# One inference step of a hybrid decoder trunk: split weights outside the experts, interleaved element by element

## What is computed

```python
# layer 0
q, fl, v, gate = split(rmsnorm(x) @ hgrn_w_in, 4)          # 1024 x 4096
o = recurrence(silu(q), 1 - f, v, log f)                   # f from fl
x = x + (headnorm(o) * g_norm * silu(gate)) @ hgrn_w_out   # 1024 x 1024
xn = rmsnorm(x)
x = x + (silu(xn @ ffn_w1) * (xn @ ffn_w3)) @ ffn_w2       # 1024 x 3584, twice, and 3584 x 1024
# layer 1
b, c, h = split(rmsnorm(x) @ conv_w_in, 3)                 # 1024 x 3072
x = x + (b * conv3(c * h)) @ conv_w_out                    # 1024 x 1024
x = x + sum over 8 experts of gate_e * swiglu(rmsnorm(x), w1[e], w3[e], w2[e])
y = rmsnorm(x)
```

## Time and profile before

| | |
|---|---|
| median of three runs (lowest, highest) | 1505.19 us (1504.82, 1506.57) |
| the profiled execution's own time | 1508.43 us |
| its span, first to last instruction | 1506.6 us |
| mean granted TensorE clock | 0.995 |
| busy: TensorE matmuls, weight loads | 1479.1 us, 1297.6 us |
| busy: VectorE, ScalarE, GpSimd | 1236.9 us, 962.0 us, 83.8 us |
| moved by DMA | 483.97 MB, 321 GB/s |

### The profile page before, as it was taken

How to read it: one execution, slowest core, us unless ns; L and a number is a source line. 1 busy time by engine, 2 the same in 40 slices (tenths; PEclk the granted TensorE clock), 3 DMA queues, 4 the chain that set the end, 5 groups by cost and what they waited for, 6 DMA issues and landing times.

```text
span 1506.6 us, 23455 instructions
## 1 busy us (share of the span) xinstructions
PE 1479.1 (98%) x8803; PEld 1297.6 (86%) x8804; DVE 1236.9 (82%) x906; ACT 962.0 (64%) x693; POOL 83.8 (6%) x65
## 2 busy tenths in 40 slices
PE   9998999999999999999999999999999999999997
PEld 8987899999999978888888888888888888888885
DVE  6898866656578779889888888888888888988987
ACT  6644353333353567777777777777777777777774
POOL 1035200000000030000000000000000000000300
PEclk9999999999999999999999999999999999999998
DMA  8745697888654669999999999999999999999990
GB/s 311 225 131 157 221 342 267 305 297 300 228 182 168 228 227 413 403 367 389 376 381 382 373 393 375 377 385 376 382 392 359 387 395 361 388 385 364 407 413 36
DMA packets 212938, 483.97 MB, mean 321 GB/s; under 512 B 8810, under 2 KB 26314, under 8 KB 209820
## 3 DMA queue, kind: packets, MB, share of 16 engines
q1 hardware_dynamic: 209224, 473.67, 85.2%
q10 hardware_dynamic: 2388, 5.32, 1.0%
q0 software_dynamic: 1280, 4.33, 0.7%
HBM read 446.45 MB, written 36.87 MB: 321 GB/s over the span
## 4 chain that ended last, share of the span: by engine, by line
PE 86%; DVE 1%; issue 0%; ACT 0%; DVEq 0%
PE Q L2544 20%; PE Q L2495 14%; PE Q L2497 14%; PE Q L2496 14%; PE Q L2039 7%; PE Q L2040 7%; PE Q L2041 7%; PE Q L2528 2%; DVE wlo L1174 1%; PE Q L2474 0%; PE Q L2505 0%; ACT yrows L1149 0%; PE Q L2400 0%; PE Q L2408 0%; PE Q L2032 0%
## 5 line engine op out<-in xcount | busy, mean ns | idle before, releaser
L1174 DVE TENSOR_TENSOR wlo<-raw,whi 128x2048 fp32r<-128x2048 f32 x413 | 940.3, 2297 | 186.2 <-ACT whi L988 109.3
L988 ACT ACTIVATE whi<-raw 128x2048 fp32r<-128x2048 f32 x336 | 642.2, 1919 | 169.8 <-PE Q L2497 81.1
L2495 PE MATMUL Q<-whi,xgh 128*128 128x512 f32 x896 | 354.2, 395 | 0.0
L2497 PE MATMUL Q<-whi,xgl 128*128 128x512 f32 x896 | 349.6, 390 | 0.0
L2496 PE MATMUL Q<-wlo,xgh 128*128 128x512 f32 x896 | 348.9, 389 | 0.0
L2039 PE MATMUL Q<-xh,whi 128*128 128x264 f32 x1024 | 294.7, 288 | 5.4 <-DVEq L1285 1.8
L2040 PE MATMUL Q<-xl,whi 128*128 128x264 f32 x1024 | 292.0, 285 | 0.0
L2041 PE MATMUL Q<-xh,wlo 128*128 128x264 f32 x1024 | 290.7, 284 | 0.0
L2039 PEld LDWEIGHTS Q<-xh,whi 128*128 128x128 f32 x1024 | 193.8, 189 | 8.1 <-issue 4.1
L2497 PEld LDWEIGHTS Q<-whi,xgl 128*128 128x128 f32 x896 | 168.1, 188 | 35.8
L2496 PEld LDWEIGHTS Q<-wlo,xgh 128*128 128x128 f32 x896 | 168.5, 188 | 33.6
(11 more groups left out here) (286 smaller groups left out, 1138.8 us busy)
## 6 DMA issues: line engine op xcount, KB each, us to landing
raw<-in_moe_w SPq DMA_DIRECT2D x336, 1024.0 KB, 7.1
raw<-in_ffn_w SPq DMA_DIRECT2D x42, 1024.0 KB, 7.3
raw<-in_hgrn_w_in SPq DMA_DIRECT2D x16, 1024.0 KB, 7.3
xg_rows<-zeros SPq DMA_DIRECT2D x6, 2048.0 KB, 10.9
y_rows<-zeros SPq DMA_DIRECT2D x6, 2048.0 KB, 11.7
raw<-in_conv_w_in SPq DMA_DIRECT2D x12, 1024.0 KB, 5.4
raw<-in_hgrn_w_out SPq DMA_DIRECT2D x4, 1024.0 KB, 5.0
raw<-in_conv_w_out SPq DMA_DIRECT2D x4, 1024.0 KB, 5.1
```

The costliest lines, as they stand in the source:

```text
L988: a.activation(bufs(q)[0], raw[:, n % RAW, PW * (q % 2):PW * (q % 2 + 1)], ACT.Copy).then_inc(hi_done, 1)
L1174: v.tensor_tensor(low, raw[:, slot, PW * half:PW * (half + 1)], high.bitcast(F32), ALU.subtract).then_inc(lo_done, 1)
L2495: t_.matmul(out, xgh[:, kt, :], high[:, w], start=(kt == 0), stop=False)
L2497: mm = t_.matmul(out, xgl[:, kt, :], high[:, w], start=False, stop=(kt == DT - 1))
```

## The change

The two tiles `whi` and `wlo` become one tile `wp` with a last axis of 2: for each slot, element and pair, the high part stands at the even and the low part at the odd position. The names `whi` and `wlo` are now views of it, so that every use outside the experts, which is written with these names, has a step of 8 bytes from one float to the next. For the experts a second tile `wm` lies over the same memory, with the two parts of a slot one behind the other, and `bufs` uses it for slots 0 to 2; there each part is contiguous as before. A slot covers the same 16 KB in both readings. The three slots of the experts' own, `whi2` and `wlo2`, stay. No instruction is added, removed or moved.

```diff
--- before.py
+++ after.py
@@ -90,8 +90,10 @@
 
         raw_at = top[0]
         raw = keep("raw", [P, RAW, CW])
-        whi = keep("whi", [P, SPLIT, PW], F32R)
-        wlo = keep("wlo", [P, SPLIT, PW], F32R)
+        w_at = top[0]
+        wp = keep("wp", [P, SPLIT, PW, 2], F32R)
+        wm = at("wm", [P, SPLIT, 2, PW], F32R, w_at)
+        whi, wlo = wp[:, :, :, 0], wp[:, :, :, 1]
         xT_at = top[0]
         xT = keep("xT", [P, DT, T])
         xn_at = top[0]
@@ -230,7 +232,7 @@
         def bufs(q):
 
             b = MOE_SLOT[q % SPLIT_M]
-            return (whi[:, b, :], wlo[:, b, :]) if b < SPLIT else (
+            return (wm[:, b, 0, :], wm[:, b, 1, :]) if b < SPLIT else (
                 whi2[:, b - SPLIT, :], wlo2[:, b - SPLIT, :])
 
         Q = [ctx.enter_context(nc.psum_tensor(f"Q{i}", [P, 4, 512], F32)) for i in range(2)]
```

## The result

The changed kernel takes 1511.87 us in the median of 7 runs (1509.91 to 1514.26), the kernel before 1505.19 in 7 runs beside it (1504.50 to 1507.86). The ratio is 1.004 with a 95% interval of 1.0028 to 1.0052: slower by 6.0 us, between 4.2 and 7.8. On another chip, against 20 runs of the kernel before with median 1506.37, the changed kernel took 1510.92 and the ratio was 1.0025 (1.0015 to 1.0035). So the change costs 0.25 to 0.4%, some 4 to 6 us. The predicted 1505 us and "no change" are wrong; the measured time lies in the range of 1502 to 1530.

A forecast was written before the change was run, and what follows sets the result against it. The prediction took TensorE's queue as the bound, with the moving operand's stream and not the load setting the pace. Its four points summed to 0 + 0 + 0 + 0, so 1505 us, with a range from 1502 to 1530.

The forecast's parts named there:

- no change: Whole kernel: the likeliest case, 1503 to 1507 us, chance 0.74, with 1505 us as the predicted time.
- Point 1, weight loads: 3744 dense matmuls outside the experts load stepped blocks: bounded by 0 and +341 to 397 us, taken as 0.
- the row that it leaned on: Transposes' loads of unstepped 4-byte floats, 139 to 140 ns: read as 0.44 ns a column, 16 bytes in 1.76 ns.
- the argument by rates: Dense weight loads: a stepped load must cross 16 bytes in 1.68 ns, nearly the rate seen on both read sides.
- the doubling of +341 to 397 us: Dense weight loads: a load taking twice as long a column becomes the bound, 1846 to 1902 us, chance 0.10.
- the cover: Dense matmuls: a load of some 106 ns lies 15 ns under the 121.2 ns between two matmuls.
- The signs: Dense loads at 188 to 189 ns would show the forecast right, loads above about 204 ns point 1 wrong.
- the small penalty: Dense loads 13 to 27 ns longer, slightly over their cover: 0 to 100 us, around 1550 us, chance 0.07.
- Point 2, VectorE: VectorE's subtractions outside the experts, stepped reads and writes: 0 to 0.5 us more per 2048 elements, taken as 0.
- Point 3, ScalarE: ScalarE's stepped copies outside the experts: between 0 and a doubling (+1.7 us each), taken as 0.
- Point 4, experts: Expert slots 0 to 2 keep each part contiguous, with steps and lengths as before: 0, stage stays at 953 us.
- The rival on VectorE and ScalarE: Either engine slower on its stepped side, unhidden in the first 200 us: 1508 to 1530 us, chance 0.06.

The follow-up runs named there:

- narrow_step1: Kernel before, with the second and third matmul of each dense group of three streaming only 128 of 264 columns, loads without a step: 1502.69 us, ratio 0.9967.
- load_step2: Kernel before, with only TensorE's weight loads outside the experts stepping by 8 bytes: 1511.49 us against 1507.4, ratio 1.003.
- experts_too: Changed kernel, with the experts' slots 0 to 2 interleaved too, so their moving operand steps by 8 bytes: 1966.39 us, ratio 1.3055 to the kernel before.
- write_step2: Changed kernel, with ScalarE and VectorE still stepping but TensorE loading 128 floats without a step: 1506.6 us, ratio 1.0004 to the kernel before.
- write_again: Second run of the changed kernel in which TensorE loads without a step while ScalarE and VectorE step: 1507.23 us, ratio 1.0005 to the kernel before.
- narrow_step2: Kernel before, with two of three dense matmuls streaming 128 of 264 columns and weight loads stepping by 8 bytes: 1521.61 us, ratio 1.0095.

## Why the prediction was wrong, by its own steps

*What bounds the kernel* held: TensorE's queue, and in the dense stage the pace of one matmul. The statement that the stream alone sets this pace in both stages was too strong. It rested on the first matmul of line 2613 behind a stream of 512 columns, where a load has over 100 ns to spare, and says nothing on 264 columns. There the load is close behind: 121.1 ns against a floor of 108.5 to 111.2 (narrow_step1).

*Point 1, weight loads, is the step that failed.* "Between these I take 0" costed the stepped load at 0, where it is 8 ns a load and 1.4 ns a matmul, 5.2 us in all. Three things went wrong.

First, the row that it leaned on doesn't carry it. The transposes' loads last 139 ns, which was read as 0.44 ns a column. A load of 128 columns would then occupy the loader for 56 ns, but the transposes of line 2528 follow one another at 0.44 / 4 us, some 110 ns:

```profile
561.27 0.44 PE Q L2528 x4
```

Whether their load or their stream sets that distance no run shows; in either case the duration is no proof of a reading side that is twice as fast.

Second, the argument by rates, 16 bytes in 1.68 ns asked for and 1.67 to 1.76 seen, was taken to mean no cost at all. It was right about the size that mattered, and rules out the doubling of +341 to 397 us. But the floor rose from 108.5 to 111.2 ns to 117 to 118. Divided by the 16-byte stretches that a load touches, the distances of loads are 117 to 118 / 64, 173.9 / 96 and 233.2 / 128, each 1.81 to 1.84 ns a stretch (241.0 / 128 = 1.88 with a step of 32 bytes). At 1.82 ns a stretch, and not the 1.67 of the argument and of rule R, the step of 8 bytes costs what was measured. This was fitted afterwards, and no further run tests it.

Third, the cover was taken as all or nothing: a load costs nothing until it is 15 ns longer. Measured, the cover is 10 to 13 ns, so the 8 ns stay within it, the new floor of 117 to 118 is still under the stream's 121.1, and yet the pace is 122.5. In the kernel before, the distances of two matmul starts from 260 to 420 us scatter from 115 to 130 ns, and 202 of 1318 are 118 or less; in the changed kernel they go from 118 to 131, and 2 of 1303 are 118 or less. So the short distances are gone. Lifting them to 119 is worth only 0.3 ns a matmul by my estimate from these counts. Where the rest of the 1.4 comes from the runs don't show, only that the stepped loads alone bring it about (load_step2).

The signs didn't fit either case. Loads at 197 to 198 ns are above "188 to 189" and below the "204" that was to tell of a fault in point 1.

The gap between "costs 0" and "costs 27 ns" was bracketed, with the small penalty at 0.07 and a typical time of 1550 us. That rival had the right mechanism and too high a price: half or all of 0.84 ns for each further stretch of 16 bytes, where it is 8 / 32 = 0.25. A loss of this size, just over what a measurement can tell, had no case of its own.

*The Trainium skill's rule* (SBUF — State Buffer, Specifications: lines of 16 bytes, at least two hits on a line for full bandwidth) fits the load roughly: two floats in 16 bytes cost 8 ns and not 0, fewer cost 72 (step of 12 bytes) and 141 (16 bytes). For the moving operand of 32-bit floats it doesn't hold: with the same two floats in 16 bytes the stream runs at half rate (experts_too).

*Point 2, VectorE:* right, 2297 ns before and after, although two of its three operands step.

*Point 3, ScalarE:* the duration was wrong, as 0 was taken and 210 ns a copy came, 0.10 ns an element, within the bounds. Its cover held everywhere, in the first 200 us too: the medians of write_step2 and write_again are within 0.1% of the kernel before.

*Point 4, experts:* right. Copies at 1919 ns, subtractions at 2288 to 2298, loads at 188, and 953 us full of matmuls as before.

*The rival on VectorE and ScalarE* (1508 to 1530 us) names a time near the measured one, but for the wrong reason. That the measured time lies in the stated range is luck: the range goes above 1507 us only for this rival, which write_step2 rules out.

## What to carry to other kernels

Before a step is put into an operand of a matmul, count the 16-byte stretches that it touches: in these runs one took TensorE some 1.8 ns (1.81 to 1.84 for stepped loads, 452.9 / 256 = 1.77 for the stream). Keep the streamed operand without a step, and let a stationary operand step by 8 bytes at most, which cost 0.25 to 0.4% here. An operation that overlaps another isn't free up to the point where the two are equal: 8 ns more under a cover of 10 to 13 cost 1.4. Its floor is read by shrinking the other one (here fewer columns) and from the distance of two starts, not from the operation's duration or slope, and not from a mean over operations of which some aren't bound by it.

## What the runs showed of the hardware that was not expected

- Two loads of a stationary block of 128 floats a partition come at least 108.5 to 111.2 ns apart, and 117 to 118 with a step of 8 bytes (narrow_step1, narrow_step2). With steps of 12, 16 and 32 bytes the load is the bound of the matmuls' pace, at 173.9, 233.2 and 241.0 ns.
- A matmul that streams 512 floats comes 226.7 ns after the one before it without a step and 452.9 with a step of 8 bytes, which leaves a stationary operand nearly as fast.
- ScalarE writes every second float 0.10 ns an element slower outside the experts (2122 against 1912 ns for 2048) and 0.06 in experts_too (2045 against 1919); VectorE reads and writes every second float at an unchanged 2297 ns.
